# Updating the inverse and its transpose each by a matmul of its own, in place of turning one into the other

## The reference

```python
def rwkv7_scan(r, decay, k, v, kk, a):
    def step(state, inp):
        r_t, w_t, k_t, v_t, kk_t, a_t = inp
        s_kk = jnp.einsum('bhvk,bhk->bhv', state, kk_t)
        state = (state * w_t[:, :, None, :]
                 - s_kk[..., None] * (kk_t * a_t)[:, :, None, :]
                 + v_t[..., None] * k_t[:, :, None, :])
        return state, jnp.einsum('bhvk,bhk->bhv', state, r_t)
    ...
    _, out = lax.scan(step, jnp.zeros((B, H, N, N), jnp.float32), tuple(xs))
```

## Time and profile before

| | |
|---|---|
| median of 3 runs | 4182.26 us (4171.77 to 4189.27) |
| the profiled execution's own time | 4182.26 us |
| its span in the trace | 4180.5 us |
| TensorE matmul busy | 3834.0 us (92%) |
| VectorE busy | 2178.2 us (52%) |
| ScalarE busy | 1560.1 us (37%) |
| GpSimd busy | 1098.3 us (26%) |
| granted TensorE clock, mean | 0.948 of full |

### The profile page before, as it was taken

The page is one execution under the profiler, slowest core; times in us unless marked ns, Lnnn a source line. Parts: engine busy times, 40 slices in busy tenths (PEclk is TensorE's granted clock), DMA queues, the critical chain, the costliest instruction groups (busy, mean ns, idle before and its releaser), DMA issues.

```text
span 4180.5 us, 46395 instructions
## 1 busy us (share of the span) xinstructions
PE 3834.0 (92%) x17487; PEld 3019.2 (72%) x17487; DVE 2178.2 (52%) x2235; ACT 1560.1 (37%) x1935; POOL 1098.3 (26%) x574
## 2 busy tenths in 40 slices
PE   7998999999999899999898997987899997986899
PEld 5865888757887768886587775676687775675777
DVE  5534666326665356663465443536545443537554
ACT  3454343334342433435533321243333322243343
POOL 6600748205564038470083000120000000020000
PEclk9999999999999999999999998998999998998999
DMA  7733767446674257673474542202454542201454
GB/s 242 232 95 126 247 205 242 143 118 230 223 231 167 77 187 246 205 234 88 146 248 149 173 135 74 101 11 91 152 192 153 180 139 83 87 30 61 151 186 136
DMA packets 493251, 649.61 MB, mean 155 GB/s; under 512 B 16075, under 2 KB 393442, under 8 KB 493090
## 3 DMA queue, kind: packets, MB, share of 16 engines
q1 hardware_dynamic: 472356, 569.62, 42.1%
q0 software_dynamic: 19584, 75.50, 5.1%
q10 hardware_dynamic: 1150, 2.29, 0.2%
HBM read 646.29 MB, written 1.05 MB: 155 GB/s over the span
## 4 chain that ended last, share of the span: by engine, by line
issue 61%; POOLq 18%; PE 12%; POOL 6%; SPq 1%; ACT 1%; DVE 0%; DMA 0%; DVEq 0%; ACTq 0%
POOLq L573 7%; POOLq L575 6%; POOLq L577 5%; PE bank L1196 4%; PE bank L897 3%; POOL mod_zone L580 2%; POOL modrow L580 1%; PE bank L1318 1%; PE bank L1329 1%; POOL modrow L562 1%; POOL mod_zone L562 1%; PE bank L869 1%; PE bank L876 0%; PE bank L877 0%; PE bank L878 0%
## 5 line engine op out<-in xcount | busy, mean ns | idle before, releaser
L2011 DVE TENSOR_TENSOR wproj_lo<-wproj,wproj_hi 128x2048 fp32r<-128x2048 f32 x252 | 745.7, 2996 | 132.9 <-ACT wproj_hi L1547 132.9
L897 PE MATMUL bank<-wproj_hi,x_hi 128*128 128x512 f32 x2112 | 542.3, 399 | 32.5 <-DVE arena L2102 22.7
L897 PE MATMUL bank<-wproj_lo,x_hi 128*128 128x512 f32 x2112 | 534.4, 396 | 0.0
L897 PE MATMUL bank<-wproj_hi,x_lo 128*128 128x512 f32 x2112 | 524.5, 391 | 0.0
L897 PEld LDWEIGHTS bank<-wproj_hi,x_hi 128*128 128x128 f32 x2112 | 399.4, 191 | 128.8 <-issue 38.6
L1587 ACT CAST actT_hi<-bank 128x512 fp32r<-128x512 f32 x132 | 77.4, 587 | 1112.0 <-PE bank L924 1112.0
L537 POOL TENSOR_SCALAR rstd<-sumsq 128x1 f32<-128x1 f32 x38 | 7.5, 197 | 1830.3 <-ACT tok L1530 1830.1
L1547 ACT CAST wproj_hi<-wproj 128x2048 fp32r<-128x2048 f32 x252 | 469.9, 1911 | 15.6 <-DMA wproj<-in_ffn_w_gate_up 15.6
L897 PEld LDWEIGHTS bank<-wproj_hi,x_lo 128*128 128x128 f32 x2112 | 399.0, 189 | 84.1
L897 PEld LDWEIGHTS bank<-wproj_lo,x_hi 128*128 128x128 f32 x2112 | 387.6, 188 | 76.6
L876 PE MATMUL bank<-wdown_hi,actT_lo 128*128 128x512 f32 x1056 | 422.2, 400 | 6.0 <-DVE actT_lo L2108 6.0
(11 more groups left out here) (417 smaller groups left out, 5246.2 us busy)
## 6 DMA issues: line engine op xcount, KB each, us to landing
wproj<-in_ffn_w_gate_up SPq DMA_DIRECT2D x336, 512.0 KB, 6.0
wdown<-in_ffn_w_down SPq DMA_DIRECT2D x132, 1024.0 KB, 5.0
wproj<-in_w_in SPq DMA_DIRECT2D x52, 1024.0 KB, 6.4
wproj<-in_ffn_w_gate SPq DMA_DIRECT2D x84, 512.0 KB, 4.8
wproj<-in_ffn_w_up SPq DMA_DIRECT2D x84, 512.0 KB, 6.4
mod_zone<-in_mod_w POOLq DMA_DIRECT2D x36, 1024.0 KB, 6.3
modrow<-in_mod_w POOLq DMA_DIRECT2D x36, 1024.0 KB, 6.0
wproj<-in_sb_w_qkv SPq DMA_DIRECT2D x48, 512.0 KB, 5.4
```

Of the source, the lines that this page charges most:

```text
L897: last = nc.tensor.matmul(proj_ps[t][:, :], rounded(x_part[of_x](c)[:, toks]), rounded(w_part[of_w][:, c, :]), start=start and c == 0, sto ...
L2011: V.tensor_tensor(rounded(wproj_lo[w.odd][:, cols]), src[:, cols], wproj_hi[w.odd][:, cols], ALU.subtract).then_inc(cols_lo, 1)
```

## The change

The turn of the inverse is dropped. `corrections(s)` makes a second product in all levels but the last: X y into one bank, beside y' invT into another. VectorE subtracts both, first from `inv` and then from `invT`, and one event tells of both. The four banks that held two corrections and two turned tiles now hold two pairs of corrections. ScalarE's copy to `inv` goes away, and with it both semaphores of the turn; the next level's product waits for VectorE's event in its place.

```diff
@@ TensorE @@
                     i, u = divmod(s, 4)
                     if i:
-                        pe.wait_ge(*inv_copied.at(l, "copy", s - 4))
+                        pe.wait_ge(*rw_v.at(l, "x", s - 4))
@@ corrections @@
                     pe.wait_ge(*rw_act.at(l, "yc", s))
                     if s >= 2:
                         pe.wait_ge(*rw_v.at(l, "x", s - 2))
+                    z_ps = down_ps[2 * (s % 2):2 * (s % 2) + 2]
                     for q in range(4):
-                        last = nc.tensor.matmul(down_ps[s % 2][:, q * P:(q + 1) * P], y_sb[u][:, q, :],
-                                                invT[u][:, q, :], start=True, stop=True)
+                        cols = slice(q * P, (q + 1) * P)
+                        if i < LV - 1:
+                            nc.tensor.matmul(z_ps[0][:, cols], invT[u][:, q, :], y_sb[u][:, q, :], start=True,
+                                             stop=True)
+                        last = nc.tensor.matmul(z_ps[1][:, cols], y_sb[u][:, q, :], invT[u][:, q, :], start=True,
+                                                stop=True)
                     last.then_inc(*rw_z.next("z"))
-
-                def turn_inverse(s):
-
-                    pe.wait_ge(*rw_v.at(l, "x", s))
-                    if s >= 2:
-                        pe.wait_ge(*inv_copied.at(l, "copy", s - 2))
-                    for q in range(4):
-                        last = nc.tensor.transpose(down_ps[2 + s % 2][:, q * P:(q + 1) * P], invT[s % 4][:, q, :],
-                                                   ident[:, :])
-                    last.then_inc(*inv_turned.next("turn"))
...
                     corrections(s)
-                    if 1 <= s <= 4 * (LV - 1):
-                        turn_inverse(s - 1)
@@ ScalarE @@
                 for s in range(4 * LV):
-                    if 3 <= s < 4 * (LV - 1) + 3:
-                        act.wait_ge(*inv_turned.at(l, "turn", s - 3))
-                        nc.scalar.copy(inv[(s - 3) % 4].rearrange("p q n -> p (q n)"),
-                                       down_ps[2 + (s - 3) % 2][:, :]).then_inc(*inv_copied.next("copy"))
@@ VectorE @@
                 for s in range(4 * LV):
+                    i, u = divmod(s, 4)
                     v.wait_ge(*rw_z.at(l, "z", s))
-                    x = invT[s % 4].rearrange(q_n)
-                    V.tensor_tensor(x, x, down_ps[s % 2][:, :], ALU.subtract).then_inc(*rw_v.next("x"))
+                    z_ps = down_ps[2 * (s % 2):2 * (s % 2) + 2]
+                    if i < LV - 1:
+                        x = inv[u].rearrange(q_n)
+                        V.tensor_tensor(x, x, z_ps[0][:, :], ALU.subtract)
+                    x = invT[u].rearrange(q_n)
+                    V.tensor_tensor(x, x, z_ps[1][:, :], ALU.subtract).then_inc(*rw_v.next("x"))
```

More of the change, by code:

```diff
@@ L437, in program @@
         rw_y, rw_z = Events(sem("rwkv_y"), ("y", 4 * LV)), Events(sem("rwkv_z"), ("z", 4 * LV))
-        inv_turned = Events(sem("inverse_turned"), ("turn", 4 * (LV - 1)))
-        inv_copied = Events(sem("inverse_copied"), ("copy", 4 * (LV - 1)))
         rw_act = Events(sem("rwkv_scalar"), ("lora_in", 1), ("lora_out", 1), ("kk_norm", 1), ("vtok_c", 1),
```

## The result

The changed kernel takes 4217.03 us in the median (4210.68 to 4227.34, 6 runs), the kernel before 4180.88 (4171.77 to 4192.13, 6 runs): ratio 1.0086, 95% interval 1.0064 to 1.0108. It is slower by 36 us, where 17.8 were forecast and 4213 was the upper end of the range. Six further runs of it on another occasion gave 1.0067 (1.0049 to 1.0084). The profiled execution took 4215.57 us, span 4213.8 us.

What follows compares the result with a forecast made beforehand. TensorE was taken to bound the loop at 0.1113 us a record. Per layer +160 - 80 = 80 records, 8.90 us; two layers 17.8 us, so span 4198.3 and, with 1.8 us around it, 4200.1 us (+0.43%); range 4188 to 4213.

Steps and rivals of the forecast that it cites:

- What bounds the loop: Both correction loops, 49.87 us each: TensorE without idle time, 448 records at 0.1113 us each.
- The removed and added work: TensorE in the loop, per layer: 80 transpose records removed (-8.90 us), 160 matmul records added (+17.81 us).
- The fourfold faster transpose: Loop's transposes by the skill's rule: step grows by 0.67 us, estimate 4209; not used; cheaper-transpose rival's chance 0.03.
- VectorE: One more subtraction of 0.69 us in 20 steps, hidden behind TensorE; as the bound (rival), 4232 us, chance 0.03.
- The dropped copies: 20 copies of 0.58 us on ScalarE removed from the loop, lying beside TensorE's work: worth 0.
- the last sentences of the sum: Behind the loops: everything starts that much later, so all 17.8 us reaches the end, 4200.1 us.
- the term for the clock behind the loop: Stretches behind both loops: expected about as long as before, 98.9 and 109.1 us, no clock cost added.
- one more such stretch in each layer: Rival behind the loops: another half-clock stretch per layer, 9.5 us in all, so 4209.6; longer fall's chance 0.11.
- The fast rival: Behind the loops: fuller loop leaves the clock up, 45.9 us back if full all through, 4154; chance 0.03.

Runs made afterwards that it cites:

- 2.2 us of padding: Kernel before with 20 matmul records that nobody reads behind each loop: 4201.98 us, ratio 1.0041.
- fills: Unread 512-column matmul ahead of both waits of each half behind the loop: kernel before 4172.37 us, ratio 0.9980; changed kernel 4191.38 us, ratio 1.0026.
- twelve records of padding: Kernel before with 12 matmul records that nobody reads behind each loop: 4191.45 us, ratio 1.0020.
- half dose: Kernel before with the turn made as a matmul in the odd steps only, 40 records more in a loop: 4192.95 us, ratio 1.0024.

## Why the prediction was wrong, point by point

**What bounds the loop** was right: no idle time on TensorE, the time is records times their distance. **The removed and added work** was right: the loop lasts 59.0 against 58.8 us, and the growth is 9.12 a layer where 8.90 was predicted, so 18.2 in place of 17.8 us, within 3%. Transposes cost half of a matmul call, as their row said: made as matmuls they give the changed kernel's time. The fourfold faster transpose (the Trainium skill, "TensorE: Matmul & The Clock Gate", Terms) doesn't fit here: 4 records against 8 at one distance is twofold. **VectorE** was right: 0.69 and 0.68, hidden, and the kernel with its double work but without the added records has the time of before. **The dropped copies** at 0: right by the same run.

**The step that failed** is the last sentences of the sum: what stands behind the loop "starts that much later" and is otherwise the same, "so all of it reaches the end". I had named the stretches behind the loops and said "about as long as before, 98.9 and 109.1 us". They became 106.2 and 116.6: the term for the clock behind the loop was set to nothing and measured 7.3 + 7.5 = 14.8 us between the two first traces. Loops and clock together are 33.1 us, and the two profiled executions differ by 33.3. (Inside of that two other items cancel: the loop began 9.1 us later, and 8.9 us came back between and behind the layers. The delay arises early: in the first 130 us TensorE is busy 94 us against 103, at a clock of 0.91 against 0.95; which of the two leads isn't shown. Up to the loop all kernels are alike, and in the 14 traces its first product starts anywhere from 2703.0 to 2720.5 us; that is scatter, not the change.) The rival was on the list, "one more such stretch in each layer", with a chance of 0.11 and 9.5 us. Its chance was too small and its price too low: the new falls last 13.7 us each (in the first layer from about 2801.4 to 2815.0 us), where I had taken the 9 and 10 us of the earlier trace rows, and half of 2 x 13.7 is 13.7 us.

**Why I gave it 0.11.** I took the falls as something that would strike both kernels alike, since "where a fall lies isn't tied to this loop alone". The runs show that it moves with the start of the short products. In the first layer: no second fall without a delay (three traces) or with 1.3 us, a second fall with 2.2 us of padding, with 4.6 us, and with 9.1 us (three traces), none with 10.5. So a shift of a few us, which I passed on as it was, moved a stretch from one pattern to the other. In the second layer the delay alone doesn't decide: without one the second fall is there in two of three traces. What goes with it in both layers is where the first fall begins. In the 20 stretches traced without fills it begins 3.4 to 6.6 us behind the first short product. Where it begins at 4.2 to 4.6 us (seven stretches) no second fall follows; where it begins at 5.4 to 6.0 us (eight), or at 3.4 to 3.5 and lasts 13.7 us (three), one does; the other two, both with twelve records of padding, begin at 6.4 and 6.6 us and have one fall only. That is what the traces have together, not a cause that a run has tested. Since the kernel before has some of these second falls itself, the mean excess is less than 14.8 us: over all executions the clock's part is some 13 us, and the four ratios of kernels with 9.1 us of delay and of the half dose give +28 to +36 us and +10 us against 18.2 and 9.1 of pure records.

**The fast rival** spoke of the clock staying up. It did not through the fuller loop, but the cost it pointed at is real: with filled waits the changed kernel comes down from 28 to 36 us above the unfilled kernel before to 11.

**Open.** Why the first fall begins where it does, the same in every trace of a kernel in the first layer and not in the second; the falls further behind (in the third branch, where VectorE is busy more than TensorE) and their price; and what exactly of the two waits and the narrow records between them the clock answers to.

## What to carry to other kernels

Added work in a stage that is bound by TensorE costs its records at their distance, and here that could be read to 3%. But look at the granted clock behind the stage too: a stretch of narrow matmuls with short waits may stand at the edge of a fall. Here a shift of 2.2 us in each layer cost about 13 us beyond its own work, as much as the clock's part of the whole change. To tell such a part from the work, set the mean clock of every execution beside its time. The remedy was cheap here, a wide matmul that nobody reads in each short wait: it made the kernel before 0.2% faster, while the change lost 0.7 to 0.9%.

## What the runs showed of the hardware that wasn't expected

- The clock fell to 1.2 GHz just before 2765.0 us in the kernel before, behind a loop without idle time on TensorE and one wait of 0.68 us; a second wait, of 0.78 us, lies within the fall. The Trainium skill ("TensorE: Matmul & The Clock Gate", Why this matters for your kernels) warns of long idle gaps between bursts; in the traces without fills no gap between the loop and the first fall is over 0.8 us, so they ask for more care than that.
- Filling only the second wait shortened the fall from 10.2 to 3.4 us; filling both took it away.
- Eighty transpose records among 448 left the loop at 1.00; the loop with none is at 1.00 as well.
- Forty records of nothing, twenty behind each loop, 4.5 us of work in the whole kernel, cost 17 us.
